# Modulation columns of a two-layer trunk: 160 one-column products, or block transposes, row sums and 12 strip products

## What is computed

```python
mx = jnp.split((jax.nn.silu(c) @ w_mod[layer] + b_mod[layer])[:, None, :], N_MOD, axis=-1)
mc = jnp.split(jax.nn.silu(c_ctx) @ w_mod[layer] + b_mod[layer], N_MOD, axis=-1)
hx = modulate(rmsnorm(x, norm_mix[layer]), mx[0], mx[1])
hc = modulate(rmsnorm(ctx, norm_mix[layer]), mc[0], mc[1])
...
x = x + mx[2] * (fx @ w_o)
x = x + mx[5] * swiglu(modulate(rmsnorm(x, norm_ffn[layer]), mx[3], mx[4]),
                       ffn_w1[layer], ffn_w3[layer], ffn_w2[layer])
```

## Time and profile before

| | |
|---|---|
| time of three runs | 2489.59, 2491.22 (median), 2496.49 us |
| the profiled execution | 2485.69 us, its span 2483.8 us |
| instructions in the profile | 33401 |
| PE busy | 2341.4 us (94%) |
| DVE busy | 1451.8 us (58%) |
| POOL busy | 1070.4 us (43%) |
| ACT busy | 623.0 us (25%) |
| mean granted TensorE clock | 0.979 of full speed |

### The profile page before, as it was taken

How to read it: one execution, slowest core, us unless ns; L and a number is a source line. 1 busy time by engine, 2 the same in 40 slices (tenths; PEclk the granted TensorE clock), 3 DMA queues, 4 the chain that set the end, 5 groups by cost and what they waited for, 6 DMA issues and landing times.

```text
span 2483.8 us, 33401 instructions
## 1 busy us (share of the span) xinstructions
PE 2341.4 (94%) x12131; PEld 1866.0 (75%) x12131; DVE 1451.8 (58%) x2482; ACT 623.0 (25%) x1018; POOL 1070.4 (43%) x815
## 2 busy tenths in 40 slices
PE   5999999999878999999999989999999989999998
PEld 3878888888534788888888878876555557888886
DVE  4584778784586368877876646545467655111113
ACT  3202354343595131000000133223212202200002
POOL 2343343344553425463554344344211035666664
PEclk8999999999998999999999999999999999999999
DMA  7753342344540344444444213344333112333332
GB/s 274 216 174 100 100 128 85 113 161 138 186 133 24 85 76 111 119 119 125 112 119 119 80 48 121 128 155 133 100 98 110 47 43 84 93 94 101 93 93 85
DMA packets 390134, 280.98 MB, mean 113 GB/s; under 512 B 31106, under 2 KB 355228, under 8 KB 390012
## 3 DMA queue, kind: packets, MB, share of 16 engines
q1 hardware_dynamic: 334220, 203.61, 28.3%
q10 hardware_dynamic: 55792, 75.71, 9.0%
HBM read 237.21 MB, written 42.07 MB: 112 GB/s over the span
## 4 chain that ended last, share of the span: by engine, by line
PE 60%; DVE 6%; issue 1%; ACT 1%; DMA 0%; POOL 0%; DVEq 0%; ACTq 0%; SPq 0%; POOLq 0%
PE PS L895 44%; PE PS L1394 3%; PE PS L1565 3%; PE PS L1406 3%; PE PS L1517 2%; PE PS L836 1%; PE PS L1485 1%; PE PS L904 1%; DVE xcr L2349 1%; PE PS L830 0%; PE PS L1349 0%; PE PS L1466 0%; DVE rdiag L2278 0%; DVE hh L2920 0%; DVE hh L2918 0%
## 5 line engine op out<-in xcount | busy, mean ns | idle before, releaser
L715 POOL TENSOR_TENSOR w_hi<-w_raw,ones 128x128 fp32r<-128x128 f32 x244 | 153.2, 628 | 1246.1 <-DMA w_raw<-in_ffn_w 432.8
L895 PE MATMUL PS<-act_hi,w_hi 128*128 128x512 f32 (+1 forms) x1824 | 656.7, 360 | 21.9 <-DVE act_lo L2308 11.3
L895 PE MATMUL PS<-act_lo,w_hi 128*128 128x512 f32 (+1 forms) x1824 | 639.8, 351 | 0.0
L895 PE MATMUL PS<-act_hi,w_lo 128*128 128x512 f32 (+1 forms) x1824 | 636.3, 349 | 0.0
L718 POOL TENSOR_TENSOR w_lo<-w_raw,w_hi 128x1024 fp32r<-128x1024 f32 (+1 forms) x244 | 594.6, 2437 | 20.4
L895 PEld LDWEIGHTS PS<-act_hi,w_hi 128*128 128x128 f32 x1824 | 348.1, 191 | 76.8 <-issue 17.7
L895 PEld LDWEIGHTS PS<-act_lo,w_hi 128*128 128x128 f32 x1824 | 347.7, 191 | 46.1 <-issue 1.2
L895 PEld LDWEIGHTS PS<-act_hi,w_lo 128*128 128x128 f32 x1824 | 346.0, 190 | 47.5
L2251 DVE SCALAR_TENSOR_TENSOR mf_acc<-mf_ring,cs,mf_acc 128x128 f32<-128x128 f32 x784 | 277.8, 428 | 2.0
L716 POOL TENSOR_SCALAR w_hi<-w_raw 128x896 fp32r<-128x896 f32 (+1 forms) x244 | 245.7, 1007 | 0.0
L2531 DVE SCALAR_TENSOR_TENSOR xT<-PS,modv,xT 128x512 f32<-128x512 f32 (+1 forms) x120 | 74.9, 657 | 233.1 <-PE PS L895 204.0
(11 more groups left out here) (352 smaller groups left out, 3569.8 us busy)
## 6 DMA issues: line engine op xcount, KB each, us to landing
w_raw<-in_ffn_w SPq DMA_DIRECT2D x120, 512.0 KB, 3.9
mf_ring<-in_w_mod SPq DMA_DIRECT2D x56, 512.0 KB, 4.0
w_raw<-in_a_w_in SPq DMA_DIRECT2D x44, 512.0 KB, 4.1
proj<-stage ACTq DMA_DIRECT2D x44, 384.0 KB, 3.9
w_raw<-in_b_w_up SPq DMA_DIRECT2D x32, 512.0 KB, 4.6
m_ring<-in_w_mod SPq DMA_DIRECT2D x12, 1024.0 KB, 8.6
rows<-g_d SPq DMA_DIRECT2D x16, 768.0 KB
m_raw<-in_w_mod SPq DMA_DIRECT2D x4, 2048.0 KB, 12.4
```

Source lines behind the costliest of these rows:

```text
L715: pool.tensor_tensor(w_hi[:, s, 0], w_raw[:, s, 0], ones[:], ALU.mult)
L895: last = pe.matmul(to[:, c0:c1], w[:, s, k, :], x[:, k, c0:c1], start=k == 0 and w is w_hi and x is hi, stop=k == kt - 1 and w is w_lo)
```

## The change

PE no longer sums over the partitions tile by tile. After the 16 operations of a tile, DVE transposes the accumulator in blocks of 32x32 (`dve.transpose`, into the first 2 x 128 or 2 x 256 columns of the tile's own ring buffer, whose weights have been used), and then sums each block's rows over 32 elements (`dve.tensor_reduce`). Of 128 partitions this leaves four partial sums, one for each strip of 32 partitions, kept in `mpart` (12 x 16 columns) or `fpart` (56 x 8 columns). Later PE multiplies them by `strips`, a 128x32 matrix made of four identities of 32x32, which adds the four strips: four small matmuls (`strip_sums`), one for each 32 rows of the result, in bank 7. It does this three times: after four steps of the first mixed unit (48 columns), after k = 2 of the first unit of down00 (16 columns, for the first 8 tiles), and at the same place of down02 (96 columns). DVE then adds the bias once for each of these (`modulation`).

The waits change with it. DVE's products no longer wait for `mm_done`; they are bound by their loads alone. PE no longer waits for `m_put` or `mf_put` at each unit. It waits at the three places for all units to be read out (`evac`) and for the accumulations of all the tiles. The buffer of a tile comes free two operations later (MOD_STEPS is 18, before 16). `fold_strips` makes `strips` in four small operations of DVE, twice, since the memory is used by others in between.

```diff
 MOD_UNITS = 12
+LATE_UNITS = 56
+MOD_STEPS = 2 * KD + 2
 MOD_LATE = 40
...
+        mpart = nc.alloc_sbuf_tensor_at("mpart", [P, MOD_UNITS, 16], F32, offset=zst_at + 15360)
+        fpart = nc.alloc_sbuf_tensor_at("fpart", [P, LATE_UNITS, 8], F32, offset=zst_at)
+        strips = nc.alloc_sbuf_tensor_at("strips", [P, 32], F32, offset=zst_at + 16128)
...
-                            sp.wait_ge(m_step, (n - 2 * RING + 1) * (2 * KD))
+                            sp.wait_ge(m_step, (n - 2 * RING + 1) * MOD_STEPS)
...
                     for k in range(kt):
                         pe.wait_ge(ready, ready0 + k + 1)
                         for s in range(together):
                             last = tile_products(s, k, kt, hi, lo, n)
-                            if late and n0 >= LATE0 and k in (4, 6):
-                                late_columns(n0 // RING, s, k)
+                            if late and s == 0 and k == 2:
+                                pe.wait_ge(evac, n0)
+                                late_columns(*late)
                             if k == kt - 1:
                                 last.then_inc(mm_done, 1)
...
+                        if late and s == 3:
+                            pe.wait_ge(m_put, 2 if name == "down00" else 3)
...
-            def late_columns(r, s, k):
-
-                if k == 4:
-                    pe.wait_ge(mf_step, (r * RING + (s + 1 - LATE0)) * (2 * KD))
-                v = k // 2 - 2
-                pe.matmul(PS[:, mod_col(s) + v:mod_col(s) + v + 1], mf_acc[:, s % 2, v, :], ones[:, 0:1],
-                          start=False, stop=False, skip_group_check=True)
...
+            def strip_sums(n, parts):
+
+                for b in range(4):
+                    last = pe.matmul(bank(7)[32 * b:32 * b + 32, 0:n], strips[:], parts(b), start=True, stop=True)
+                last.then_inc(m_mm, 1)
+
+            def late_columns(u0, u1):
+
+                pe.wait_ge(mf_step, u1 * MOD_STEPS)
+                strip_sums(2 * (u1 - u0), lambda b: fpart[:, u0:u1].rearrange("p u (v b) -> p u v b", v=2)[:, :, :, b])
+
...
-                    if late and k in (4, 6):
-                        late_columns(r, s, k)
-                    if name in WITH_MOD and not (isinstance(r, int) and r == 0) and k % 2 == 0:
-
-
-                        if k == 0:
-                            pe.wait_ge(m_step, (r * RING + (s - RING + 1)) * (2 * KD))
-                        m, v = k // 4, k // 2 % 2
-                        pe.matmul(PS[:, mod_col(s) + k // 2:mod_col(s) + k // 2 + 1], m_acc[:, s % 2, v, m * P:m * P + P],
-                                  ones[:, 0:1], start=False, stop=False, skip_group_check=True)
...
-            dense(5)
+            dense(4)
+            pe.wait_ge(evac, 16)
+            pe.wait_ge(m_step, MOD_UNITS * MOD_STEPS)
+            strip_sums(4 * MOD_UNITS, lambda b: mpart[:].rearrange("p u (v m b) -> p u m v b", v=2, m=2)[:, :, :, :, b])
+            dense(1)
             gla_gates(0, 0)
...
             def mod_products(r, s):
 
 
-                step0 = (r * RING + (s - RING)) * (2 * KD)
-                if not (isinstance(r, int) and r == 1 and s < 2):
-                    dve.wait_ge(mm_done, r * RING + (s - 1))
+                step0 = (r * RING + (s - RING)) * MOD_STEPS
                 dve.wait_ge(m_in[s], r * 16)
                 for k in range(KD):
...
                         ins.then_inc(m_step, 1)
-
-            def late_products(r, s, first=False):
-
-
-                step0 = (r * RING + (s - LATE0)) * (2 * KD)
-                if not first:
-                    dve.wait_ge(mm_done, r * RING + (s - 1))
+                blocks = m_ring[:, s, 0:2].rearrange("p a c -> p (a c)")
+                dve.wait_ge(m_step, step0 + 2 * KD)
+                dve.transpose(blocks, m_acc[:, s % 2].rearrange("p v c -> p (v c)")).then_inc(m_step, 1)
+                dve.wait_ge(m_step, step0 + (2 * KD + 1))
+                u = r * RING + (s - RING)
+                out = mpart[:, u] if isinstance(u, int) else mpart[:, bass.ds(u, 1), :].rearrange("p a c -> p (a c)")
+                dve.tensor_reduce(out, blocks.rearrange("p (b i) -> p b i", i=32), AX.X, ALU.add).then_inc(m_step, 1)
+
...
-
-            def late_unit(r, s):
-
...
-                m = r * RING + (s + MOD_LATE - LATE0)
-                dve.tensor_tensor(modv[:, bass.ds(m, 1), :], PS[:, mod_col(s):mod_col(s) + 2].unsqueeze(1),
-                                  ptab[:, 0, bass.ds(m, 1)].unsqueeze(2).broadcast_to([P, 1, 2]), ALU.add).then_inc(mf_put, 1)
...
+                u = r * RING + (s - LATE0)
+                blocks = mf_ring[:, s % 2, 0:2].rearrange("p a c -> p (a c)")
+                dve.wait_ge(mf_step, step0 + 2 * KD)
+                dve.transpose(blocks, mf_acc[:, s % 2].rearrange("p v c -> p (v c)")).then_inc(mf_step, 1)
+                dve.wait_ge(mf_step, step0 + (2 * KD + 1))
+                out = fpart[:, u] if isinstance(u, int) else fpart[:, bass.ds(u, 1), :].rearrange("p a c -> p (a c)")
+                dve.tensor_reduce(out, blocks.rearrange("p (b i) -> p b i", i=32), AX.X, ALU.add).then_inc(mf_step, 1)
+
+            def fold_strips():
+                chain(dve.tensor_copy(strips[:], ident[:, 0:32]))
+                for g in (1, 2, 3):
+                    chain(dve.tensor_tensor(strips[:], strips[:], ident[:, 32 * g:32 * g + 32], ALU.add))
+
+            def modulation(m0, m1, sums):
+
+                dve.wait_ge(m_mm, sums)
+                chain(dve.tensor_tensor(modv[:, m0:m1, :], bank(7, 2 * (m1 - m0)).rearrange("p (m x) -> p m x", x=2),
+                                        ptab[:, 0, m0:m1].unsqueeze(2).broadcast_to([P, m1 - m0, 2]), ALU.add), m_put)
...
-            def next_products(r, s):
-                mod_products(*((r, s + 1) if s + 1 < RING else (r + 1, 0)))
-
-            def mod_both(r, s):
-                next_products(r, s)
-                mod_unit(r, s)
-
-            mod_products(1, 0)
-            each_ring(dve, RING, 2 * RING, mod_both)
-            for s in range(RING):
-                if s + 1 < RING:
-                    next_products(3, s)
-                mod_unit(3, s)
-            dve.wait_ge(m_put, MOD_UNITS)
+            fold_strips()
+            each_ring(dve, RING, MOD_UNITS, mod_products)
+            modulation(16, MOD_LATE, 1)
             scales(0, 1)
...
                             if not (last and s == RING - 1):
                                 late_products(*((r, s + 1) if s + 1 < RING else (r + 1, 0)))
                             body(r, s)
-                            if s % 2 == 0:
-                                dve.wait_ge(fsg_done, r * 2 + (s // 2 - n0 // 2 + before + 1))
-                            late_unit(r, s)
                         return both
...
-                        dve.wait_ge(mf_put, 8)
+                        modulation(MOD_LATE, MOD_LATE + 8, 2)
...
                         each_ring(dve, n0 + count - RING, RING, with_late(True))
-                        dve.wait_ge(mf_put, 56)
+                        modulation(MOD_LATE + 8, MODS, 3)
...
                 out = sel[:, 32 * k:32 * k + 8]
                 for g in range(4):
                     chain(dve.tensor_tensor(out, out, ident[:, 32 * g + 8 * k:32 * g + 8 * k + 8], ALU.add))
+            fold_strips()
             norm("ffn0", T)
             ffn(0, T)
```

53 lines of the change are left out of this document (15 added, 38 removed).

## The result

| | before | changed kernel |
|---|---|---|
| median | 2489.9 us (7 runs) | 2473.7 us (7 runs, 2467.9 to 2482.1) |
| profiled execution (span) | 2485.7 (2483.8) us | 2471.7 (2470.0) us |
| mean granted clock | 0.979 | 0.966 |

The ratio is 0.9933, with a 95% interval of 0.9913 to 0.9952: 16 us faster, where 40 had been forecast. The time lies inside the range, 22 us from the value.

What follows compares the result with a forecast made beforehand. The prediction took PE, busy 94% of the span, as the bound. Terms of -17.8 us (qkv) and -22.1 us (FFN of layer 0) made -39.9 us, so 2451.3 us from a median of 2491.2, range 2443 to 2475.

Steps and rivals of the forecast that it cites:

- The pace of a one-column product: In PE's FFN timeline: each one-column product costs PE 0.22 us, so removing it gains that much.
- the whole qkv term: In qkv: 48 products and 9.2 us of waits go, strips and set-up come; sum -17.8 us, no stall.
- the price of both pieces: In layer 0's FFN: transpose and row sum at 0.48 us each, 0.97 us a unit with the hand-over.
- rival 2: In qkv and FFN: transpose and row sum twice as slow a column, +15.5 us, 2467 us; chance 0.15.
- nine us of room: At qkv's strips: DVE ends at 205 us, PE asks at 214.4, so PE does not stall.
- Rival 3: End of qkv: splits hold DVE fully, it ends at 223, PE waits 9 to 11 us; 2462 us, chance 0.1.
- the FFN term: In layer 0's FFN: products and waits removed, less strips, fold and 4.8 us given back; sum -22.1 us.
- I take the middle, -1: In up00: between 3.3 us lost and 5.8 us gained, a middle of -1, giving back 4.8 us.
- In up01, DVE's 29.6 idle us cover 8 x 1.64: In up01: idle time absorbs 13.1 us of added DVE work and PE's quickening by 7.0 us.
- +0.8 for the fold: Before layer 0's FFN norm: building the strips' matrix takes four small DVE additions, +0.8 us.
- Rival 4: In FFN and qkv: DVE becomes the bound, with transposes at the reciprocal's price; 2519 us, chance 0.05.
- One sign of a wrong forecast that I had named: In up01: PE waiting for the weights' split would say that DVE's lag reaches the SP queue.

Runs made afterwards that it cites:

- e1: Only the qkv part of the change, put into the kernel before: 2475.1 us, ratio 0.9913 to the kernel before.
- e2: Only the part in the FFN of layer 0, put into the kernel before: 2486.8 us, ratio 0.9972 to the kernel before.
- e4: Changed kernel with layer 0's FFN modulation tiles loaded one unit later in SyncE's order: 2453.0 us, ratio 0.9829 to the kernel before.
- e12: e4 with the second building of the strips' matrix moved into up00's slack ring: 2454.1 us, ratio 0.9841 to the kernel before.
- e8: Kernel before plus a transpose and row sum after each of 56 FFN modulation units, results unused: 2512.4 us, ratio 1.0067.
- e6: Changed kernel without the 56 transposes and 56 row sums of layer 0's FFN, sums left out: 2453.0 us, ratio 0.9837 to the kernel before.
- e14: Changed kernel with GpSimd's low-part subtraction in layer 0's FFN made a one-input copy: 2456.0 us, ratio 0.9834 to the kernel before.
- e7: Changed kernel with layer 0's FFN transpose and row sum made once for two units: 2494.2 us, ratio 0.9998 to the kernel before.
- e16: e12 with the high parts of most FFN up weights rounded on ScalarE, not GpSimd: 2464.7 us, ratio 0.9880 to the kernel before.

## Why the forecast was wrong

**Right.** The pace of a one-column product, 0.22 us; the whole qkv term (-17.8; the gates' lead is 17.7, e1 gives -17.6 by the medians and -22 by the ratio); the price of both pieces (0.97 forecast, 0.92 a unit), so that rival 2 did not come. That PE does not wait at qkv's strips was luck in part: nine us of room were forecast and 0.4 were left, since PE came 4.6 us earlier than thought and DVE 4.4 later. Rival 3, DVE late there at the forecast prices, was that close.

**Wrong: the FFN term, -22.1, measured -6 to -7 by itself (e2).** Inside the whole change it is less: 16 us in all, with 17.7 already gained at the gates. By stage the sum had about -1, -7 and -5 for up00, up01 and up02 and -10 for the down stretches (an estimate from its terms); the two profiles differ by +4.0, +6.7, -0.8 and -19.0. Three steps of it:

1. *"I take the middle, -1"* for up00. The two estimates behind it were +3.3 (bare addition, 18.8 us a pair) and -5.8 (GpSimd's work hidden in the new pieces). The pair measured 18.75 us over the last five of up00 (924.28 to 1018.03): the bare addition, to 0.05 us. There was no ground for a middle: e4 and e12 have pairs of 16.2 to 17.4 us and of 18.4 to 19.9 and few between, and the mean of two such states is none of them.
2. *"In up01, DVE's 29.6 idle us cover 8 x 1.64"*. This was the costly one. Only 12.7 us of that idle time was waiting for PE, and part of it existed because the splits drifted through the pairs: in the kernel before, up01's first chain takes 6.5 to 7.4 us in the first four pairs, with part of a split outside it, and 8.6 to 9.1 in the last three, which have as little room as up00. In the changed kernel it takes 8.8 to 9.4 from the second pair on. Once DVE is the slower one, the loads leave by its steps, and both splits stay on the first chain. DVE's busy time in a pair went from 14.0 to 16.8 us, 2.8 more where 1.64 had been counted (estimates from the stage rows: 112.4 and 127.7 of 142 us, by pairs of 17.68 and 18.73). Up01 alone grew 6.7 us where a gain of 7.0 had been counted. e8 shows it without the rest of the change, e6 the size of the pieces, e14 GpSimd's part.
3. *+0.8 for the fold.* 3.9 in the profile, not measurable at the end.

**The rivals.** Rival 4 had the right mechanism, DVE as the bound, but I gave it 0.05, since I tied it to a slow transpose, when 0.5 us of room in the pair of the earlier trace rows against 1.64 of new work decided it at the ordinary price. The sign of the FFN term stayed a gain only since the down stretches gave 19 us. What the Trainium skill, SBUF — State Buffer, section Who interferes with whom, says of the row sum agrees with its own rows (0.42 us with a split beside it, e4; 419 to 422 ns in all 56 of the changed kernel), but freed time helps only if a split falls there.

One sign of a wrong forecast that I had named did come: PE waits for the weights' split in up01, once, 5.5 us. And PE waits at the strips of down02, 4.2 us, where I had said none.

## What to carry to other kernels

When an edit moves work from a full engine to one with 0.5 us of room a period, add durations period by period and don't spend idle time that exists only because the other engine is slower. If an added piece turns the bound around, what it triggers can lock to it, as the splits did here; look for the phase (here: which instruction the contending transfers and splits land on) and forecast its states apart. Then try the order of the loads first: here it was worth 23 to 26 us, more than the change itself, with no compute instruction added.

## What the runs showed that I had not expected

- The same instructions take 16.2 or 18.7 us a pair, and the state can persist through a stage or switch inside it. What makes it switch is open.
- A 0.46 us GpSimd piece took 1.66 to 2.04 us when it met an unheld chain of multiply-adds (e4's up02): the hold goes both ways.
- Less work on the bound engine made the kernel slower (e7, +0.65% against the changed kernel, with the loads shifted too), and work moved to an idle engine did (e16 against e12, +0.4%).
- A transpose of 128x256 in f32 took 445 to 448 ns and a row sum 256 to 8 419 to 422 ns in all 56, whether a split ran beside them or not; both are below a multiply-add of that width (median 481 in the changed kernel). So the row sum is not the slowest DVE operation here, against the rule cited in the prediction; the measurement decides.
